# Eight modulation slabs summed over their blocks on VectorE, one product with ones each, and an eleventh slab buffer

## What is computed

```python
sh1, sc1, g1, sh2, sc2, g2 = split(silu(c) @ w_mod + b_mod, 6)        # modulation, also for c_ctx
hx = rmsnorm(x, norm1_g) * (1 + sc1) + sh1                            # hc likewise from the context
u, q, k, v, lf, lb, g, gate = project(hx, w_in, ...)                  # 1024 -> 5664
o = gla_bidirectional(q, k, v, lf, lb, state of the context)          # 4 heads, gated linear attention
x = x + g1 * mixer_out(pool(u), o, g, gate, ...)
x = x + g2 * hier_moe(rmsnorm(x, norm2_g) * (1 + sc2) + sh2, ...)     # 32 experts, top 2 of 8 in a group
```

## Time and profile before

| | |
|---|---|
| median of 3 runs | 1368.38 us |
| span of the profiled execution | 1365.8 us |
| PE busy | 1195.7 us (88%) |
| DVE busy | 651.7 us (48%) |
| ACT busy | 485.2 us (36%) |
| HBM read | 369.74 MB, 271 GB/s over the span |

### The profile page before, as it was taken

How to read it: one execution, slowest core, us unless ns; L and a number is a source line. 1 busy time by engine, 2 the same in 40 slices (tenths; PEclk the granted TensorE clock), 3 DMA queues, 4 the chain that set the end, 5 groups by cost and what they waited for, 6 DMA issues and landing times.

```text
span 1365.8 us, 22197 instructions
## 1 busy us (share of the span) xinstructions
PE 1195.7 (88%) x9435; PEld 923.8 (68%) x9435; DVE 651.7 (48%) x991; ACT 485.2 (36%) x695; POOL 0.2 (0%) x4
## 2 busy tenths in 40 slices
PE   5999999999867665766666799999999999999997
PEld 4677788887434333333333599878888799888886
DVE  4445446786111010210201467576666767766665
ACT  5552246554101000000000346454444456554443
POOL 0000000000000000000000000000000000000000
PEclk9999999999998878988998999999999999999999
DMA  9757666579999999999999972436364444554520
GB/s 342 258 194 249 229 231 245 196 279 380 428 419 428 429 429 425 428 429 428 428 428 428 391 256 99 150 123 246 133 238 150 176 155 155 185 204 166 223 86 31
DMA packets 89116, 371.95 MB, mean 272 GB/s; under 512 B 6491, under 2 KB 8329, under 8 KB 76365
## 3 DMA queue, kind: packets, MB, share of 16 engines
q1 hardware_dynamic: 87480, 369.73, 69.0%
q10 hardware_dynamic: 1556, 1.08, 0.3%
HBM read 369.74 MB, written 1.05 MB: 271 GB/s over the span
## 4 chain that ended last, share of the span: by engine, by line
PE 68%; DMA 24%; DVE 3%; ACT 2%; issue 1%; SPq 1%; ACTq 0%; DVEq 0%
DMA arena<-in_moe_w 20%; PE ring L2034 8%; PE ring L2478 7%; PE ring L2023 5%; PE acc L2126 4%; PE acc L2127 4%; PE acc L2128 4%; PE ring L2036 4%; PE ring L2025 2%; DMA arena<-in_w_mod 2%; PE acc L2007 2%; PE acc L2009 1%; PE acc L2008 1%; DMA arena<-in_moba_w_qkv 1%; PE ring L2172 1%
## 5 line engine op out<-in xcount | busy, mean ns | idle before, releaser
L2478 PE MATMUL ring<-arena 128*32 128x256 f32 x2048 | 152.2, 463 | 76.2 <-DMA arena<-in_moe_w 76.2
L2478 PEld LDWEIGHTS ring<-arena 128*32 128x32 f32 x2048 | 79.5, 132 | 144.5 <-issue 72.8
L1280 DVE TENSOR_TENSOR wlo<-arena,whi 128x2048 fp32r<-128x2048 f32 x56 | 128.0, 2290 | 50.6 <-ACT whi L839 50.6
L1704 DVE TENSOR_TENSOR arena<-arena,ring 128x128 f32<-128x128 f32 x32 | 12.2, 380 | 258.7 <-ACT arena L1084 258.7
L1084 ACT ACTIVATE arena<-ring 128x128 f32<-128x128 f32 x32 | 8.9, 277 | 349.2 <-PE ring L2478 349.2
L839 ACT ACTIVATE whi<-arena 128x2048 fp32r<-128x2048 f32 x56 | 106.8, 1910 | 43.7 <-PE acc L2128 25.4
L2034 PE MATMUL ring<-xboth,whi 128*128 128x512 f32 x320 | 113.8, 398 | 0.0
L2036 PE MATMUL ring<-xboth,wlo 128*128 128x256 f32 x320 | 89.8, 281 | 0.0
L2497 PE MATMUL ring<-arena 128*32 128x256 f32 x1024 | 62.1, 382 | 29.7 <-DVE arena L1707 27.7
L2497 PEld LDWEIGHTS ring<-arena 128*32 128x32 f32 x1024 | 31.7, 109 | 58.1 <-DVE arena L1707 31.8
L2034 PEld LDWEIGHTS ring<-xboth,whi 128*128 128x128 f32 x320 | 60.1, 188 | 14.6
(11 more groups left out here) (418 smaller groups left out, 2654.8 us busy)
## 6 DMA issues: line engine op xcount, KB each, us to landing
arena<-in_moe_w SPq DMA_DIRECT2D x94, 2048.0 KB, 21.1
arena<-in_mlp_w_in SPq DMA_DIRECT2D x16, 2048.0 KB, 10.3
arena<-in_mlp_w_out SPq DMA_DIRECT2D x16, 2048.0 KB, 7.8
arena<-in_w_mod SPq DMA_DIRECT2D x11, 2048.0 KB, 8.3
arena<-in_w_in SPq DMA_DIRECT2D x11, 2048.0 KB, 9.3
arena<-in_moba_w_qkv SPq DMA_DIRECT2D x6, 2048.0 KB, 19.5
arena<-in_dil_w_qkv SPq DMA_DIRECT2D x4, 2048.0 KB, 8.9
arena<-in_w_gla_br SPq DMA_DIRECT2D x2, 2048.0 KB, 7.9
```

The lines of the kernel that those rows point to most:

```text
L1280: dve.tensor_tensor(lo, raw, hi.bitcast(F32), ALU.subtract).then_inc(G["split_ready"], 1)
L2478: ins = pe.matmul(o, xs[:, kt, j, :], w[kt][g], start=(kt == 0), stop=(kt == KT - 1))
```

## The change

Slabs 4 to 11 no longer go through PE's `mod_rows`. DVE computes the sum over the 8 blocks itself: the first block times its column of silu(c), then seven times block times column plus the sum so far, each waiting for the one before (`mod_sum`). One product of 32 bit operands with a matrix of ones then sums over the partitions and spreads the result (`mod_bc`). The two 2 KB rows of partial sums are used alternately. ACT has no part in it any more. The steps of `mod_sum` are put into DVE's stream at chosen places, three of them in two pieces.

The scratch that is reserved in SBUF at build time is cut to 1024 bytes per partition, and an eleventh slab buffer of its own takes its place. Odd modulation slabs from 5 on use it, even ones buffer 2. Then it holds w2 of expert 0 (requested ahead of `pool_br` 0) and after it belongs to the six buffers in turn, where buffer 0 leaves them. Eleven expert slabs are placed ahead of the first use. The second block's slabs use buffers 0, 3, 1, 2.

```diff
+OWN_SLOT = 10
-MIXER_SLOT.update({("mod", s): 1 if s == 9 else 2 for s in range(4, 12)})
+MIXER_SLOT.update({("mod", s): OWN_SLOT if s % 2 else 2 for s in range(4, 12)})
...
-    order += [("mod_rows", 4, "V"), ("v", 0, "A"), ("v", 1, "A")]
+    order += [("v", 0, "A"), ("v", 1, "A")]
...            (likewise every other ("mod_rows", 5 to 11) of bank_plan)
-RING, AHEAD = 4, 10
-AHEAD_SLOTS = (3, 6, 0, 1, 5, 2, 4, 7, 8, 9)
-MOE_SLOTS = (6, 3, 0, 5, 1, 2)
-LAYER_SLOTS = (0, 1, 2, 3)
+RING, AHEAD = 4, 11
+AHEAD_SLOTS = (3, 6, OWN_SLOT, 1, 5, 2, 4, 7, 8, 0, 9)
+MOE_SLOTS = (OWN_SLOT, 3, 6, 5, 1, 2)
+LAYER_SLOTS = (0, 3, 1, 2)
+SCRATCH = 1024
...
+        own = sb("own", [P, SLAB])
-        slot = [at(o, SLAB) for o in slot_at]
+        slot = [at(o, SLAB) for o in slot_at] + [own[:, :]]
...   slab_freed(n)
             else:
-                bank_use = ("mod_rows", s)
+                return G["part_ready"], KT * (s - 3)
...   SP's stream
+                if (name, s) == ("pool_br", 0):
+                    sp.wait_ge(*slab_freed(SLAB_AT["mod", 11]))
+                    load_expert(moe0 + 2, 2, 0)
...
-                elif 2 <= s < looped or s >= looped + per * (TURNS - 2):
-                    s = {3: 4, 4: 3, 6: 7, 7: 6, 8: 9, 9: 8}.get(s, s)
+                elif 3 <= s < looped or s >= looped + per * (TURNS - 2):
+                    s = {3: 9, 5: 3, 6: 5, 8: 6, 9: 10, 10: 8, 11: 12, 12: 11}.get(s, s)
...   ACT's stream: mod_rows(4) to mod_rows(11) removed
...   DVE's stream
-            def mod_low(s):
-                b = bank_of("mod_rows", s)
-                dve.wait_ge(G["modhi_ready"], s - 3)
-                dve.tensor_tensor(mod_lo, b, mod_hi.bitcast(F32), ALU.subtract).then_inc(freed["V"], 1)
+            def mod_sum(s, first, last):
+                n = SLAB_AT["mod", s]
+                w, part = view(n, KT, 512), mod_part[:, s % 2, :]
+                for kt in range(first, last):
+                    scale = scol[:, kt, 0:1]
+                    if kt:
+                        dve.wait_ge(G["part_ready"], KT * (s - 4) + kt)
+                        ins = dve.scalar_tensor_tensor(part, w[:, kt, :], scale, part, ALU.mult, ALU.add)
+                    else:
+                        dve.wait_ge(landed[SLOT_OF[n]], 16 * NTH[n])
+                        if s >= 6:
+                            dve.wait_ge(bank_full, BANK_AT["mod_bc", s - 2] + 1)
+                        ins = dve.tensor_scalar(part, w[:, kt, :], scale, None, ALU.mult)
+                    ins.then_inc(G["part_ready"], 1)
...
+            mod_sum(4, 0, 7)
             pre_lo(3)
...                                        the gates' logarithms
-            dve.tensor_copy(row_pick[:, :], C("selb")).then_inc(G["row_pick_ready"], 1)
-            mod_low(4)
+            mod_sum(4, 7, KT)
+            mod_sum(5, 0, KT)
...
             mod_bc(4)
+            mod_sum(6, 0, KT)
             pre_lo(4)
-            mod_low(5)
             mod_bc(5)
             pre_lo(5)
+            mod_sum(7, 0, KT)
             pre_lo(6)
...                                        qT scaled
             pre_lo(7)
-            mod_low(6)
...                                        factors, scaled keys and queries
             mod_bc(6)
+            mod_sum(8, 0, KT)
+            mod_sum(9, 0, 4)
             pre_lo(8)
-            mod_low(7)
+            mod_sum(9, 4, KT)
             pre_lo(9)
             mod_bc(7)
-            mod_low(8)
...                                        in the loop over the heads, after a head's masks
+                mod_sum(10 + h // 2, 4 * (h % 2), 4 * (h % 2) + 4)
                 if h != 1:
                     mod_bc(8 + max(h - 1, 0))
-                if h:
-                    mod_low(h + 8)
...   PE's stream: mod_rows(4) to mod_rows(11) removed
             def mod_bc(s):
-                moved(pe, "mod_rows", s)
                 b = bank("mod_bc", s)
-                if s == 4:
-                    pe.wait_ge(G["row_pick_ready"], 1)
-                pe.matmul(b, row_pick[:, :], mod_hi, start=True, stop=False)
-                full(pe.matmul(b, row_pick[:, :], mod_lo, start=False, stop=True))
+                pe.wait_ge(G["part_ready"], KT * (s - 3))
+                full(pe.matmul(b, ones, mod_part[:, s % 2, :], start=True, stop=True))
...
-    nc = bacc.Bacc("TRN2", target_bir_lowering=False, num_devices=1)
+    nc = bacc.Bacc("TRN2", target_bir_lowering=False, num_devices=1, dynamic_dma_scratch_size=SCRATCH)
```

More of the change, by code:

```diff
@@ L149, in bank_plan @@
     order += [("z", (tt, j), "V") for tt in range(TT) for j in range(4)]
-    order += [("mod_rows", 4, "V"), ("v", 0, "A"), ("v", 1, "A")]
+    order += [("v", 0, "A"), ("v", 1, "A")]
     order += [("cum", i, "A") for i in range(4)]
     order += [("remc", i, "A") for i in range(4)]
-    order += [("mod_bc", 4, "V"), ("mod_rows", 5, "V"), ("v", 2, "A"), ("v", 3, "A"), ("mod_bc", 5, "V"), ("qT", 0, "V"), ("qT", 1, "V")]
-    order += [("mod_rows", 6, "V"), ("v", 4, "A"), ("v", 5, "A"), ("mod_bc", 6, "V"), ("mod_rows", 7, "V"), ("v", 6, "A"), ("v", 7, "A")]
-    order += [("mod_bc", 7, "V"), ("mod_rows", 8, "V")]
+    order += [("mod_bc", 4, "V"), ("v", 2, "A"), ("v", 3, "A"), ("mod_bc", 5, "V"), ("qT", 0, "V"), ("qT", 1, "V")]
+    order += [("v", 4, "A"), ("v", 5, "A"), ("mod_bc", 6, "V"), ("v", 6, "A"), ("v", 7, "A")]
+    order += [("mod_bc", 7, "V")]
     for h in range(NH + 1):
@@ L161, in bank_plan @@
         else:
-            order += [("o", h - 1, "A")] + [("mod_bc", h + 7, "V")] * (h > 1) + [("mod_rows", h + 8, "V")] * (h < NH)
+            order += [("o", h - 1, "A")] + [("mod_bc", h + 7, "V")] * (h > 1)
     order += [("u", 0, "A"), ("u", 1, "A")] + [("g", (0, j), "V") for j in range(2)]
@@ L317, in build @@
         mod_row = at(44 * K1, 2, 512)
-        mod_hi, mod_lo = (split_at(f"mod_{what}", 44 * K1 + 512 * i, 512) for i, what in enumerate(("hi", "lo")))
+        mod_part = mod_row
         ez = [at(o * K1, 4, DK) for o in (40, 34)]
@@ L469, in build @@
         a_step = sem("scalar_step")
[L470 removed]
+        names = "x1_ready part_ready tmp_ready base_ready ssq_ready lstd_ready centred_sum ht_ready hid_ready hlow_ready hsq_ready hhi_ready hlo_ready chi_ready clo_ready prehi_ready prelo_ready pre_used kT_done kc_done kT_ready ghi_ready glo_ready yhi_ready ylo_ready mlow_ready gated mixed zhi_ready zlo_ready abs_ready L_ready lr_ones whi_ready split_ready xhi_ready xlo_ready atthi_ready chosen_ready flag_ready pick_ready put_ready dcol_ready dsilu_scaled scol_zero scol_ready square_ready nstd_ready tn_ready mod_ready c_ready exp1_ready lr_part keys_ready cross_ready h_ready ez_ready ostd_ready on_ready z_ready lg_diff rexp_ready comb_ready ssq_half out_stored eps_ready ttok_ready gain_ready s1_ready hidT_ready put_done projected rope_read rot_ready value_ready scored masked max_ready exp_ready turned_done pT_ready weighted_done att_ready share_diff share_exp scaled_ready crossed_done attlo_ready".split()
         G = {n: sem(n) for n in names}
@@ L632, in slab_freed @@
                 bank_use = {0: ("u", 1), 1: ("qT", 1), 3: ("v", 3), 4: ("v", 7)}[s]
+            elif s in MODS:
+                bank_use = ("mod_rows", s)
             else:
-                bank_use = ("mod_rows", s)
+                return G["part_ready"], KT * (s - 3)
             return bank_full, BANK_AT[bank_use] + 1
@@ L819, in mod_rows @@
             def mod_rows(s):
-                b = take("mod_rows", s)
-                if s in MODS:
-                    act.activation(mod_slot(s), b, ACT.Copy).then_inc(freed["A"], 1)
-                else:
-                    act.activation(mod_hi, b, ACT.Copy).then_inc(G["modhi_ready"], 1)
+                act.activation(mod_slot(s), take("mod_rows", s), ACT.Copy).then_inc(freed["A"], 1)
             def split_hi(h):
@@ L930, in _ @@
             act.wait_ge(G["L_ready"], 4)
-            mod_rows(5)
             pre_hi(4)
@@ L936, in _ @@
             pre_hi(6)
-            mod_rows(6)
             pre_hi(7)
@@ L940, in _ @@
             value_tokens(5)
-            mod_rows(7)
             pre_hi(8)
@@ L945, in _ @@
             pre_hi(9)
-            mod_rows(8)
             def state(h):
@@ L1380, in _ @@
                 dve.tensor_copy(kT[:, 2 * i:2 * i + 2, :], kT_bank(i).rearrange("p (h t) -> p h t", h=2)).then_inc(G["kT_ready"], 1)
+            dve.wait_ge(G["scol_ready"], 1)
+            moved(dve, "mod_cols", MODS[-1])
+            mod_sum(4, 0, 7)
             pre_lo(3)
```

11 lines of the change are left out of this document (removed).

## The result

The changed kernel takes 1377.18 us (median of 4 runs, 1376.21 to 1378.09) beside 1369.28 us of the kernel before (4 runs, 1367.79 to 1370.88): 1.0059 times as long, with an interval of 1.0045 to 1.0072. A later set of 6 runs (`after_again`) gave 1376.61 us against 1367.66 and a ratio of 1.0067 (1.0055 to 1.0079). The kernel became slower by 0.6%, a little more than forecast.

What follows compares the result with a forecast made beforehand. PE was taken to bound the mixer, transfers the experts. The terms -13.0 + 8.6 + 6.7 + 4.9 - 0.6, plus half a microsecond for a bank, gave +7.1: from 1368.38 to 1375.5 us, range 1363 to 1382 (8 in 10).

Steps and rivals of the forecast that it cites:

- PE's work: eight products less, spreads dearer: Mixer: eight products with silu(c) columns go, with a 0.6 us wait, -15.4 us; dearer spreads +2.4; work falls by 13.0.
- stall A: Ahead of values 4: PE waits for pre_lo(6), behind DVE's sum of late-landing slab 7; 9.4 us for 0.8, +8.6.
- stall B: Ahead of slab 8's spread: PE waits for the bank freed by DVE's late addition for slab 7; 7.0 us, +6.7.
- waits for slab 11 and a late bank: PE's 0.6 us wait for slab 11 goes; half a microsecond is added for the bank of slab 8.
- clock: After each of the two long PE waits the granted clock falls: 2.45 us each, +4.9, between 0 and 10.
- eleventh slab: Experts: PE's use of expert 4 sets requests of slabs 18 and 19, so one slab more gives only -0.6 us.
- What bounds the kernel: PE bounds the mixer, transfers the experts from 387 us; a microsecond of PE ahead of 387 moves the rest by one.
- PE's gain: Mixer: PE gives up eight products of 1.85 us each, spreads get dearer; its own work falls by 13.0 us.
- The spread's price: Each of eight spreads becomes one full 32 bit product of 0.86 us instead of two passes of 0.56: +2.4 us.
- The block's price: DVE's sums: first block 0.48 us, the other seven 0.68 each, 0.72 with their waits; 5.5 us a slab.
- PE's gain stands: Rival: slab 7 is in time or the sums hide; 1357 us, with the whole slab 1352; chance 14%.
- Only stall A fails to come: Rival: slab 7 of w_mod lands nearly with w_in 4, so only the other stall comes; 1365 us; chance 12%.

Runs made afterwards that it cites:

- after_again: The changed kernel without any edit, profiled a second time with 6 more runs: 1376.61 us, ratio 1.0067 to the kernel before.
- busy_early: both_in_time with nine more products of 128 columns that nobody reads, in PE's early waits near 28 and 38 us: 1351.81 us.
- both_in_time: Changed kernel, but SP requests slab 7 ahead of w_in 4, and around the heads DVE does first what PE waits for: 1355.11 us.
- before_busy_early: The kernel before with the same nine early products as busy_early: 1367.41 us, ratio 0.9996 to the kernel before.
- sum7_later: Changed kernel, but DVE sums slab 7 behind pre_lo(7) instead of ahead of pre_lo(6): 1363.57 us, 0.9955 of the kernel before.
- the first fix: Changed kernel, but DVE's addition of slab 7's spread stands ahead of slab 9's sum instead of behind pre_lo(9): 1378.73 us.
- short_blocks: Changed kernel, but seven of the eight blocks of each sum cut to 16 of 512 columns, order kept, for timing only: 1369.11 us.
- busy_in_stalls: Changed kernel with products nobody reads: eleven ahead of values 4, eight ahead of the spread of slab 8: 1372.68 us.

## Why the prediction was right

The time was forecast as 1375.5, 7.1 us above the median before; it came out 7.9 above in the first set and 8.9 in the second. Term by term, from the two first profiles. Keys end at 60.28 and 63.41 us, the last spread at 179.33 and 190.26, the experts at 770.27 and 781.10. PE's waits in the second stretch are 1.70 and 19.10 us. The work of the changed order at full clock is that of `busy_early`: 104.63 us less 0.66 of wait, 103.97, against 119.05 less 1.70, 117.35, before.

| term | forecast | measured | from |
|---|---|---|---|
| PE's work: eight products less, spreads dearer | -12.4 | -13.4 | 117.35 to 103.97 |
| stall A | +8.6 | +10.1 | 0.77 to 10.83 of wait |
| stall B | +6.7 | +7.4 | 0.32 to 7.74 |
| waits for slab 11 and a late bank | -0.1 | -0.1 | 0.61 to 0.53 |
| clock | +4.9 | +3.8 | 126.85 less 19.10 less 103.97 (second profile: +5.5) |
| eleventh slab | -0.6 | -0.1 | 590.94 to 590.84 from last spread to experts' end |
| behind the experts | 0 | -0.3 | 588.85 to 588.50 |
| start | 0 | +3.1 | the early fall |
| sum | +7.1 | +10.5 | spans 1365.8 and 1376.3 |

The second profile of the changed kernel has a span of 1378.5 us. Its two stalls are the same (10.73 and 7.74 us). Its clock term is 128.46 us less 19.00 of wait less 103.97, which is 5.5; its early fall cost 1.4 us, and the fall at 335 another 2.4.

- **What bounds the kernel** was read rightly. Between the last spread and the end of the experts lie 590.9 us before and 590.8 after, and 590.3 in `both_in_time`, where PE comes 11 us earlier than before. A microsecond of PE ahead of the last spread moved the end by one, in both directions. Where this stretch was longer, 593.1 us in `after_again` and 593.5 in `before_busy_early`, 2.4 us of it are the clock's fall at the end of the mixer.
- **PE's gain.** 1.0 us more than forecast. The spread's price was right: from its start to the next product but one pass 1.09 us in `both_in_time` (124.31 to 125.40), of which one reduced-precision product has 0.23, so the spread costs 0.86. The products with columns were worth more than 1.85 us each where reduced-precision products stand beside them. The one at 127.06 starts 0.33 us behind its neighbour instead of 0.23, and the first product behind it takes 0.34 (128.91 to 129.25) instead of 0.23. Some 0.1 us for each such change, at most of the eight places, is about the 1.0 us; this is an estimate, and no run tests it.
- **Stall A** is where and why the prediction put it, 1.5 us longer. The landing took 14.4 us instead of the 13.4 that the landing at 111.3 supposed, and a slab's sum 6.0 instead of 5.5. The request times (97.9 with 3.1 of early fall added gives 101.0, measured 100.69) and PE's end of the queries (109.7 and 3.1: 112.8, measured 112.61) were met.
- **Stall B**: 7.4 for 6.7. The eight blocks took 0.78 us apiece with their waits instead of 0.72.
- **The block's price.** I took 0.68 us from an operation with one operand in PSUM. The new one has all in SBUF and takes 0.752. The Trainium skill ("VectorE: DVE Perf Modes", the section on the TRN2 errata and SBUF sources) gives a PSUM source the larger fixed part of the two, by which the new operation should be the cheaper one. The measurement says otherwise for this operation, and it decides.
- **The clock.** The two falls are there, with 0.50 in both rows above. They cost 3.8 us together in the first profile, as most of the low spell at A lay in the wait itself: from 116.4 to 126.6, PE worked only for 3.16 us. In the second the low spells were 3 us longer each and cost 5.5. The forecast of 4.9 lies between, and the bounds of 0 to 10 held. The likeness that I took it from was weaker than I wrote: ahead of the wait at 401.6, PE was busy for only 3.87 of the 6.0 us from 386 and 3.66 of the 5.0 from 392.
- **The eleventh slab.** Its mechanism is shown: requests 18 and 19 hang on the same product of expert 4 with eleven slabs and with ten.
- **The start** is the step that was missing: no term stood for a part of the kernel that the change does not touch. It adds up to 3 us to runs of the changed kernel. Without it the first profile would have been 7.4 us above before, against 7.1. That these two are so close is in part luck: stalls A and B came 2.2 us longer, PE's own work and the clock 2.1 shorter, and in the second profile the clock and the fall at 335 would have made it 11.

The rivals: "PE's gain stands" is what `both_in_time` and `busy_early` do (1355.1 and 1351.8; the rival gave 1357 and, with the whole slab, 1352), but only after both orders are changed. "Only stall A fails to come" is `sum7_later`, 1363.6 for 1365.

## What to carry to other kernels

Work moved to an engine that is less than half busy still has a place in that engine's stream, and everything behind it in the stream waits with it: what decides is who waits for the next instructions behind each insertion, and when the operand of the inserted one lands. When one such wait is removed, follow the waiting engine on through its next uses of data and of banks; here the first fix moved 7.74 us to two other waits of 7.38. Put first what the other engine waits for (the addition, the masks), fill with the sums behind, and request the operand of an early insertion ahead of transfers that are needed later.

## What the runs showed of the hardware

- A chained operation of DVE with three operands in SBUF takes 0.234 us for 16 columns and 0.752 for 512 (`short_blocks`, changed kernel). By an estimate from the two, some 0.22 us do not depend on the columns; for 56 such blocks this is 12 us of the sums.
- The granted clock fell some time after PE's last long wait: in `both_in_time` PE waits 5.30 us until 14.0, then 0.76, 1.58 and 1.28 us between 19 and 40 us at a granted clock of 1.00, and then runs at 0.54 from 41.3 to 48.2, for 3 us of loss. With nine small products in the second and third wait (0.25 us each) the clock stayed at 1.00 in `busy_early`, where PE's waits up to then were 5.30, 0.66 and 0.46 us. The Trainium skill ("TensorE: Matmul & The Clock Gate", the section on depth-cycling as a second failure mode) tells of short idle spells between groups of products that make the clock swing between its two levels, there with PSUM banks in turn; this trace agrees as far as its short waits and its 0.54 go.
- Two runs of one program can differ in where the clock falls: the first profile of the changed kernel has 1.00 from 335.3 to 342.2 us, the second 0.51, at a price of 2.4 us.
- Products that nobody reads, placed in a wait that lasts anyway, cost nothing here (values 4 began at 123.21 instead of 123.44) and kept the clock at 1.00 (`busy_in_stalls`).
